# The 16 smallest experts of a mixture-of-experts layer in blocks of 64 rows, two matmul passes and a fold instead of three passes

## The reference, cut to what matters

```python
logits = (xt @ router_w + router_b).astype(jnp.float32)
top_val, top_idx = lax.top_k(logits, TOP_K)          # TOP_K = 4 of N_EXPERTS = 32
gate = jax.nn.softmax(top_val, axis=-1)
...
def expert_block(args):
    xblk, e = args
    hh = xblk @ w1[e] + b1[e]                        # w1[e]: 1024 x 2048
    glu = jnp.minimum(hh[:, :D_FF], SWIGLU_LIMIT)
    lin = jnp.clip(hh[:, D_FF:], -SWIGLU_LIMIT, SWIGLU_LIMIT)
    act = glu * jax.nn.sigmoid(SWIGLU_ALPHA * glu) * (lin + 1.0)
    return act @ w2[e] + b2[e]                       # w2[e]: 1024 x 1024
```

## Time and profile before

| | |
|---|---|
| median of 3 runs (lowest, highest) | 2271.85 us (2271.79, 2272.94) |
| span of the profiled execution, first to last instruction | 2269.9 us |
| TensorE busy, share of the span | 98% |
| VectorE, ScalarE, GpSimd busy | 78%, 55%, 19% |
| mean granted TensorE clock, of full speed | 0.997 |
| read from HBM | 533.79 MB |

### The profile page before, as it was taken

One profiled execution on the slowest core, in us unless ns is written; L12 is line 12 of the kernel. 1 busy time (PEld: TensorE's weight loads), 2 busy tenths in 40 slices (PEclk: granted clock), 3 DMA queues, 4 the chain that ended last, 5 costly groups with the idle time before them and its releaser, 6 DMA issues.

```text
span 2269.9 us, 30685 instructions
## 1 busy us (share of the span) xinstructions
PE 2235.8 (98%) x10681; PEld 1828.9 (81%) x10681; DVE 1768.0 (78%) x1652; ACT 1238.6 (55%) x1154; POOL 429.3 (19%) x421
## 2 busy tenths in 40 slices
PE   7999999999999999999999999999999999999998
PEld 3888888888887887888788888888888888888886
DVE  6756655555646766757899999999999999999997
ACT  6322132222225624632777777777777777777774
POOL 3000000000221132102522222222212222223222
PEclk9999999999999999999999999999999999999999
DMA  8322223131321121146899999999999999999995
GB/s 301 121 93 93 98 88 130 56 130 57 105 98 38 38 75 38 57 149 215 310 360 367 374 373 375 386 367 371 381 362 372 370 369 383 370 376 372 385 365 199
DMA packets 135516, 542.98 MB, mean 239 GB/s; under 512 B 16131, under 2 KB 24467, under 8 KB 101390
## 3 DMA queue, kind: packets, MB, share of 16 engines
q1 hardware_dynamic: 123192, 516.30, 60.1%
q0 software_dynamic: 11952, 21.44, 3.9%
q10 hardware_dynamic: 296, 4.21, 0.5%
HBM read 533.79 MB, written 26.38 MB: 247 GB/s over the span
## 4 chain that ended last, share of the span: by engine, by line
PE 95%; DMA 2%; DVE 1%; POOL 1%; ACT 0%; issue 0%; SPq 0%; POOLq 0%; DVEq 0%
PE ps L2272 90%; PE ps L2828 1%; PE ps L2840 1%; PE ps L2619 1%; POOL list_d L865 1%; DMA ar<-h_d,ar 0%; DMA ar<-in_ctx 0%; PE ps L2564 0%; DMA out_x<-ar,cur 0%; DMA raw<-in_w_mod 0%; PE ps L2510 0%; PE ps L2384 0%; DVE nmx L1875 0%; ACT hhi L1026 0%; PE ps L2717 0%
## 5 line engine op out<-in xcount | busy, mean ns | idle before, releaser
L2272 PE MATMUL ps<-whi,yhi 128*128 128x512 f32 x1072 | 346.5, 393 | 0.1
L2272 PE MATMUL ps<-hhi,yhi 128*128 128x512 f32 x1072 | 342.6, 389 | 0.0
L2092 DVE TENSOR_TENSOR hlo<-raw,hhi 128x2048 fp32r<-128x2048 f32 x132 | 302.6, 2294 | 47.3 <-ACT hhi L1333 47.3
L1333 ACT ACTIVATE whi<-raw 128x2048 fp32r<-128x2048 f32 x132 | 253.5, 1921 | 98.9 <-PE ps L2272 98.9
L2092 DVE TENSOR_TENSOR wlo<-raw,whi 128x2048 fp32r<-128x2048 f32 x132 | 298.7, 2282 | 3.4 <-ACT whi L1333 1.9
L1333 ACT ACTIVATE hhi<-raw 128x2048 fp32r<-128x2048 f32 x132 | 253.1, 1918 | 76.5 <-PE ps L2272 76.5
L1450 DVE TENSOR_TENSOR wlo<-raw,whi 128x2048 fp32r<-128x2048 f32 x56 | 128.2, 2289 | 159.5 <-ACT whi L995 159.4
L2272 PEld LDWEIGHTS ps<-whi,yhi 128*128 128x128 f32 x1072 | 201.2, 188 | 53.9 <-issue 12.1
L2272 PEld LDWEIGHTS ps<-hhi,yhi 128*128 128x128 f32 x1072 | 201.2, 188 | 41.7
L2272 PE MATMUL ps<-whi,hhi 128*128 128x512 f32 x592 | 233.3, 394 | 0.0
L2272 PE MATMUL ps<-whi,hlo 128*128 128x512 f32 x592 | 230.8, 390 | 0.0
(11 more groups left out here) (355 smaller groups left out, 4436.6 us busy)
## 6 DMA issues: line engine op xcount, KB each, us to landing
raw<-in_exp_w SPq DMA_DIRECT2D x264, 1024.0 KB, 7.7
ar<-in_exp_w SPq DMA_DIRECT2D x132, 1024.0 KB, 7.6
raw<-in_w_in SPq DMA_DIRECT2D x44, 1024.0 KB, 5.0
raw<-in_w_mod SPq DMA_DIRECT2D x22, 1024.0 KB, 6.4
raw<-in_w_br_ret SPq DMA_DIRECT2D x8, 1024.0 KB, 5.0
ar<-in_x SPq DMA_DIRECT2D x8, 512.0 KB, 7.4
raw<-in_w_br_diff SPq DMA_DIRECT2D x4, 1024.0 KB, 5.1
raw<-in_w_out SPq DMA_DIRECT2D x4, 1024.0 KB, 9.6
```

The costliest lines, as they stand in the source:

```text
L1333: act.activation(e_whi[j % ESPL], e_raw[s], ACT.Copy).then_inc(e_hi, 1)
L2092: V.tensor_tensor(e_wlo[j % ESPL], e_raw[s], e_whi[j % ESPL].bitcast(F32), ALU.subtract).then_inc(e_lo, 1)
L2272: return pe.matmul(out, lhsT, rhs, start=start, stop=stop, skip_group_check=skip)
```

## The change: what it does

The experts are ranked by their number of rows on the chip. Experts 0 and 1 always count as the two first. The 16 first ones are *wide* and keep blocks of 128 rows. The other 16 are *narrow*: blocks of 64 rows. Items 0 and 1 are wide, then narrow and wide alternate (2 narrow, 3 wide, ..., 29 wide, 30 narrow), and 31 and every extra item are narrow. An extra item now begins behind the 128th row of a wide expert or behind the 64th of a narrow one.

In a narrow item the stationary operand is 128 columns again, but 64 of them are the high parts of 64 rows and 64 are the low parts of the same rows. Two passes (times the high and times the low part of the weights) then give high x high plus high x low in the PSUM partitions 0 to 63, and low x high plus low x low in 64 to 127. A *fold* adds the lower half to the upper: ScalarE copies partitions 64 to 127 out of PSUM (`lower_up`, `lower_y`), and one matmul for each bank with a shifted identity (`fold`, 64 partitions) adds them to partitions 0 to 63.

Ranking, and the list of which expert each item is, take some 25 more small operations of VectorE in the routing, of which 9 stand ahead of the last tiles' work. SyncE reads the expert of each item from that list from item 2 on. GpSimd reads back the list of rows in two forms with two transfers.

```diff
+def narrow(b):
+    return b >= LAST or b >= 2 and b % 2 == 0
...
# SyncE
-            with sp.Fori(1, N_EXPERTS) as i:
-                for j in range(FIRST):
-                    load_w1(i, i, j)
-                for k in range(MOE_N - FIRST):
-                    load_w2(i - 1, i, FIRST + k, k)
-            sp.wait_ge(items_ready, 1)
+            for j in range(FIRST):
+                load_w1(1, 1, j)
+            for k in range(MOE_N - FIRST):
+                load_w2(0, 1, FIRST + k, k)
+            sp.wait_ge(items_ready, 2)
...
+            with sp.Fori(2, N_EXPERTS) as i:
+                extra(i)
# ScalarE
+            def glu_half(n):
+                act.wait_ge(up_full, n * 2 + 1)
+                act.activation(F(A_GS, D)[0:H], psf[0:H, 2 * COL:4 * COL], ACT.Silu, scale=ALPHA).then_inc(glu_done, 1)
...
+            def lower_up(i):
+                act.wait_ge(e_used, chunk(i, FIRST - 1) + 1)
+                for c in range(2):
+                    act.activation(low_banks[:, 2 * c:2 * c + 2, :], ps[H:P, 2 + 2 * c:4 + 2 * c, :],
+                                   ACT.Copy).then_inc(up_low, 1)
+            def lower_y(i):
+                act.wait_ge(e_used, chunk(i + 1, MOE_N - 1) + 1)
+                act.activation(low_banks[:, 0:2, :], ps[H:P, 6:8, :], ACT.Copy).then_inc(y_low, 1)
+            def item(i, half_b, half_a, half, half_n, n=None):
                 for j in range(AHEAD, ESPL):
                     hi_e(i, j)
+                if half_b:
+                    lower_y(i - 2)
+                act_high(i - 1, half_a)
                 for j in range(ESPL, MOE_N - 1):
                     hi_e(i, j)
+                if half:
+                    lower_up(i)
+                    hi_e(i, MOE_N - 1)
+                    x_high(i + 1, half_n)
+                    glu_half(n)
+                else:
+                    glu(i)
+                    hi_e(i, MOE_N - 1)
+                    x_high(i + 1, half_n)
                 for j in range(AHEAD):
                     hi_e(i + 1, j)
# VectorE
+            def x_low(n, half=False):
+                m, to = (H, xthi[:, :, H:P]) if half else (P, xtlo)
...
+            def activate_half(i, n, between):
+                dve.wait_ge(up_full, n * 2 + 2)
...
+                if half_b:
+                    give_half(i - 2, n_b)
...
+                if half:
+                    lo_e(i, MOE_N - 1)
+                    x_low(i + 1, half_n)
+                    activate_half(i, n, lambda: lo_e(i + 1, 0))
+                    lo_e(i + 1, 1)
# TensorE, up and down alike
                         mm(o, xthi[:, kk, :], wh, late and kk == 0, False)
-                        mm(o, xthi[:, kk, :], wl, False, False)
-                        last = mm(o, xtlo[:, kk, :], wh, False, kk == KC - 1)
+                        last = mm(o, xthi[:, kk, :], wl, False, half and kk == KC - 1)
+                        if not half:
+                            last = mm(o, xtlo[:, kk, :], wh, False, kk == KC - 1)
...
+            def add_low(o, low):
+                return mm(o, fold[H:P, :], low, False, True, True)
+            def fold_up(n):
+                for c in range(2):
+                    pe.wait_ge(up_low, n * 2 + c + 1)
+                    for b in (2 * c, 2 * c + 1):
+                        last = add_low(ps[:, 2 + b, :], low_bank[b])
+                    last.then_inc(up_full, 1)
+            def fold_y(n):
+                pe.wait_ge(y_low, n)
+                for c in range(2):
+                    last = add_low(ps[:, 6 + c, :], low_bank[c])
+                last.then_inc(y_full, 1)
+            def item(i, half_b, half_a, half, half_n, n=None, n_b=None):
+                if not (isinstance(i, int) and i == 1):
+                    down(i - 2, i - 1, half_b, LAST_DOWN)
+                    turn_act(i - 1, half_a)
+                def fold_before(kk):
+                    if half_b and kk == 1:
+                        fold_y(n_b)
+                up(i, half, fold_before)
                 pe.wait_ge(gathered, i * 16 + 32)
                 pe.wait_ge(act_lo, i * 2)
+                turn_x(half_n)
+                down(i - 1, i, half_a, FIRST_DOWN[:1])
+                if half:
+                    fold_up(n)
+                down(i - 1, i, half_a, FIRST_DOWN[1:])
...
             def last_down():
-                turn_act(end)
-                down(end - 1, end, LAST_DOWN)
+                down(end - 1, end, True, LAST_DOWN)
+                turn_act(end, True)
```

More of the change, by code:

```diff
@@ L48 @@
 AHEAD = 2
-BIAS_EVERY = 7
 RET_HEADS = 4
@@ L1364, in item, with item_at @@
-                x_high(i + 1)
+                if half:
[7 more added lines that the diff above has]
+                    x_high(i + 1, half_n)
                 for j in range(AHEAD):
                     hi_e(i + 1, j)
+            def item_at(i):
+                item(i, *(narrow(i + d) for d in range(-2, 2)), nth(i))
@@ new lines, in _ @@
+            tl.did(V.scalar_tensor_tensor(out=row_key, in0=ps[0:E, 3, E:2 * E], scalar=float(E), in1=row_add,
+                                          op0=ALU.mult, op1=ALU.add))
+            tl.wait()
+            tl.did(V.tensor_scalar(full[:, 1:SLOTS_H], iota[0:E, 1:SLOTS_H], float(H), count, ALU.mult, ALU.is_lt))
+            tl.did(V.tensor_scalar(above, row_key, key, None, ALU.is_gt))
+            tl.wait()
+            tl.did(V.tensor_reduce(n_full, full[:, 1:SLOTS_H], AX.X, ALU.add))
@@ new lines, in _ @@
+            tl.did(V.tensor_scalar(not_before[:, 0:NEWS], iota[0:E, 0:NEWS], before, None, ALU.is_ge))
+            tl.wait()
+            tl.did(V.scalar_tensor_tensor(out=valid[:, 0:NEWS], in0=iota[0:E, 0:NEWS], scalar=behind,
+                                          in1=not_before[:, 0:NEWS], op0=ALU.is_lt, op1=ALU.mult))
+            tl.wait()
+            V.scalar_tensor_tensor(out=part_no[:, 0:NEWS], in0=iota[0:E, 0:NEWS], scalar=step, in1=valid[:, 0:NEWS],
+                                   op0=ALU.add, op1=ALU.mult).then_inc(flag_ready, 1)
@@ L2253, in last_low @@
             def last_low():
-                act_low(end, (0,))
-                give_y(end - 1, chunk(end, MOE_N - 1))
-                act_low(end, (1,))
+                act_low(end, True, (0,))
+                act_low(end, True, (1,))
+                give_half(end - 1, end)
                 for j in range(AHEAD, ESPL):
@@ L2851, in add_bias @@
                         r = slice(b // 2 * 64, b // 2 * 64 + 64)
-                        last = mm(ps[:, 2 + b, :], sel[r, :], bias[b % 2][r], not late, False)
+                        last = mm(ps[:, 2 + b, :], (sel_half if half else sel)[r, :], bias[b % 2][r], not late, False)
                     last.then_inc(sel_used, 1)
@@ L2898, in item, with item_at @@
                 pe.wait_ge(gathered, i * 16 + 32)
                 pe.wait_ge(act_lo, i * 2)
-                turn_x()
-                down(i - 1, i, FIRST_DOWN)
+                if half_n:
+                    hold()
+                turn_x(half_n)
+                down(i - 1, i, half_a, FIRST_DOWN[:1])
+                if half:
+                    fold_up(n)
+                down(i - 1, i, half_a, FIRST_DOWN[1:])
+            def item_at(i):
+                item(i, *(narrow(i + d) for d in range(-2, 2)), nth(i), nth(i - 2) + 1 + WIDE)
```

419 lines of the change are left out of this document (256 added, 163 removed).

## The result

The changed kernel takes 2309.08 us (median of four runs, 2307.11 to 2310.56), against 2271.82 us for the kernel before on the same chip. The ratio is 1.0164, 95% interval 1.0149 to 1.0178: slower by 1.6%. I had predicted 2215 us, faster. The profiled execution has a span of 2308.3 us.

The account below looks back on a forecast made before the run. TensorE was taken to set the expert stage's pace, with VectorE and the transfers within 7% and 2% of full. Stage -62, head +1.5 and tail +4 gave -56.5, so 2215 us; 8 in 10 range 2189 to 2252.

Parts of the forecast that it names:

- (b): From the end of a narrow `up` to that of the next wide one: 36.0 us, counted on TensorE.
- (a): From the end of a wide `up` to that of the next narrow one: 29.5 us, with VectorE as the bound.
- the term of the stage: From item 1's `up` to item 32's, 31 items at 33.3 us: -62 us; the engines alone would give -85.
- The head: Added list-making operations on VectorE before the first chunk's low part: +1.5 us (0 to +4).
- The tail: Behind the last `up`, item 31's output leaves about 17 us later, not 12.7: +4 us (0 to +6).
- TensorE's work: In a narrow item 48 matmuls go, 4 + 2 for the fold come: 25.2 us instead of 35.3.
- the rival that it doesn't do what it says: More than 33 blocks come out, each costing 33 us, so two would take the gain; chance 0.03.
- (c): From one narrow `up` to the next narrow one, twice at the end: 31.3 us each, counted on VectorE.
- The fold hand-over: Between narrow and wide items, waits around ScalarE's two copies and the fold: at most 1 us per pair.
- The transfers: Weight transfers take 33.3 us per item in the expert stage, giving -62 us in place of -85; chance 0.60.
- the sign that I had named: If transfers bind, ScalarE's high parts wait for them in the profile after, which no row of before shows.
- The rival of the clock: TensorE's clock drops to the 1.2 GHz level in narrow stretches: +250 us less the remaining gain, some 2450 us; chance 0.05.

Follow-up runs that it names:

- e9_two_only: Changed kernel with VectorE waiting for its own subtraction behind chunks 4 and 9 of an item, GpSimd's order left as it was: 2222.37 us, ratio 0.9787.
- e7_half_low: Changed kernel with the selector ahead of the copy of `cur`, VectorE subtracting only half of each chunk's columns from item 2 on: 2212.32 us, ratio 0.9737.
- e8_short_copy: Changed kernel with selector moved ahead, VectorE waits behind chunks 4, 7 and 10, ScalarE copying 128 of 512 columns before the fold: 2222.84 us, ratio 0.9788.
- e6_two_gaps: Changed kernel with the selector ahead of the copy of `cur` and VectorE waiting for its own subtraction behind chunks 4 and 9: 2223.72 us, ratio 0.9795.

## Why the prediction was wrong, point by point

**The step that failed** is (b), from the end of a narrow `up` to the end of the next wide one. The prediction has the bias there at 0.9 us with no wait ahead of it, and lists as new waits only those around the fold: "At most 1 us per pair". Measured, (b) was 44.5 us for the predicted 36.0. Of the 8.5 us some 5.6 are TensorE's wait for the selector (67.1 us in 12 waits), and the rest goes with the low clock behind it (7 us at 0.53 hold some 3 us less work, by estimate). I never followed GpSimd's chain (scatter, landing, copy of `cur`, selector, bias matmuls of the next `up`), though my own (a) says what is new for it: VectorE becomes the bound, so it has no gaps. The page showed GpSimd at 19%, but low use isn't slack. Its scatter took 2.8 us in the kernel before, where a small gap of VectorE stood 1.1 to 1.3 us behind its start in every item; VectorE waited for ScalarE 155 times in 1300 to 2200 us, at about every second chunk. Where the selector was in time in the changed kernel, from item 2 to item 3, the same stretch took 36.64 us.

The Trainium skill has a rule for this (SBUF — State Buffer, "Who interferes with whom"): VectorE and GpSimd share a pair of ports as a lock, and a VectorE instruction with two SBUF inputs contends with a GpSimd instruction that reads SBUF; the one that comes second is blocked until the other is through. The scatter's row numbers lie in SBUF. By the rule it should wait for the instruction under way, 2.2 us here. The same section infers that a `tensor_tensor` doesn't hold up a transfer issued by GpSimd, and in that the runs disagree. With the rule they agree in kind (15.91 us beside an unbroken run, 2.70 with one gap in it) and go further in size: where VectorE had the next subtraction ready, GpSimd was held for seven of them in a row, and for all eight (18.04 us) where no gap came.

**The sum, term by term**, between the prediction's own boundaries. From the end of item 1's `up` to that of item 32's it took 1094.3 us before, 1123.5 after and 1034.0 in e9_two_only. So the term of the stage, predicted -62, was +29.2, and with the gaps -60.3. The head: that first `up` ended at 1141.37 before and at 1143.23 after, +1.9, predicted +1.5. The tail, from the end of the last `up` to the end of the span, was 34.2 before and 41.6 after: +7.3, predicted +4 (0 to +6). Item 31's output leaves 20.0 us behind the last `up` there, not 17. 29.2 + 1.9 + 7.3 = 38.4 us, the growth of the span (2308.3 - 2269.9 = 38.4).

**TensorE's work and (a)** were right. The records of matmuls fell by 702; 17 x 42 = 714 were predicted. (a) measured 29.35 us, predicted 29.5, and VectorE is its bound: with lighter subtractions (e7_half_low) it fell to 25.8. 33 items ran: the rival that it doesn't do what it says is out. **(b)** with the gaps is 37.45 us (e9_two_only), and there the transfers hold the pair. **(c)**, predicted 31.3 both times, took 36.2 and 31.7 us in the changed kernel (the first with 4.8 us of waiting for the selector) and 31.6 and 33.5 in e9_two_only.

**The fold hand-over**, "at most 1 us per pair", held: e8_short_copy changed the time by nothing that can be measured (2222.84 against 2224.55 us), and the stretch with the fold by 0.8 us.

**The transfers** were priced well, at 33.3 us per item against 33.6 in e6_two_gaps and e7_half_low, but the changed kernel didn't come to that bound in the mean: it moved 358 GB/s from 1300 to 2100 us. In e7_half_low ScalarE does wait for them, the sign that I had named. The limit of about 358 GB/s that the Trainium skill states (DMA: Bandwidth & Descriptors, Specifications) doesn't hold here: e7_half_low passed it by 10% at 394. That the changed kernel came out at just 358 is chance, since two gaps in VectorE's work brought it to 392.

**The rival of the clock** had the right sign and the wrong mechanism. The clock fell for some 7 us behind the standstill for the selector, and for some 3 us in the narrow `up` shown above, not over whole narrow stretches. The second fall didn't make (a) longer than predicted. Matmuls in the place of the standstill gave back 25 us over the 13 pairs, 11 net, where I had priced the rival at 250.

**With the gaps** the prediction's sum would nearly have held: 2222.37 us against 2215. Its terms in e9_two_only are -60.3 for the stage (predicted -62), +2.2 for the head and +7.8 for the tail, together -50.3 for the predicted -56.5. More than half of the 6.2 us that are missing lie in the tail, 1.7 in the stage (33.35 us per item). The changed kernel without the gaps is what was forecast, though, and there the sum failed.

**What stays open.** That a lock of ports is what holds GpSimd, the runs show only by its effect: the scatter ends 1.4 to 1.5 us behind VectorE's first gap, or behind its first instruction with an operand in PSUM. Why it doesn't get its turn between two subtractions isn't shown; the records have each start 0.08 us before the one ahead has ended (2.28 us long, 2.20 apart), so they show no free moment. The copy of two integers in each partition is long in the same places (6.82 us; mean from 1300 to 2100 us 3.8 us, in e9_two_only 1.3). Why the tail grew by more than predicted wasn't followed up. And I didn't try fewer bytes, which would be the next step now that the transfers bind.

## What to carry to other kernels

When an edit makes VectorE the bound, look at what GpSimd does beside it: small gaps that nobody planned may be all that lets it through, and they go when VectorE gets no rest. Follow the chain of every engine with low use from the end of its work to who waits for it, and price each instruction for the case that its neighbour never pauses. A scatter whose instruction, not its landing, is several times longer than elsewhere in the same trace is the sign. Two waits of VectorE on its own result mended it here for 0.3 us each.

## What the runs showed of the hardware that I hadn't expected

A GpSimd scatter beside back-to-back VectorE subtractions with both inputs in SBUF was held up for as long as they had no gap: 15.9 us for seven, up to 18.04 for eight, and 2.7 where a gap of 0.19 us came early. In the kernel before, a subtraction that started 2.32 us behind the last one instead of 2.20 was enough (2.8 us). Each time the scatter ended 1.35 to 1.5 us behind the first gap. A wait of VectorE on its own subtraction makes such a gap and costs 0.29 us. A core reading weights moved 392 to 394 GB/s over 800 us at a share of 1.01 (e6_two_gaps, e7_half_low), though the kernel before had shown a share of 0.99 at 373 in the same window: a share near 1 didn't mean that nothing more could be had. TensorE's granted clock stood at 0.53 for 7 us after 5.3 us of standing; filling the standstills with matmuls gave back 1.9 us for each pair of items.
